# A 27,000-instruction block kernel: modulation vector built in column halves, later modulation tiles in six places, second attention in single visits

## What is computed

```python
cond = jax.nn.silu(c)
for i in range(2):
    mod = (cond @ ada_w[i] + ada_b[i])                  # ada_w[i]: 1024 x 6144
    sh1, sc1, g1, sh2, sc2, g2 = jnp.split(mod, 6)      # twelve vectors of 1024 in all
    h = rmsnorm(x, norm1_g[i]) * (1 + sc1) + sh1
    y = sliding_window_sink_attention(...) if i == 0 else stick_breaking_attention(...)
    x = x + g1 * y
    h = rmsnorm(x, norm2_g[i]) * (1 + sc2) + sh2
    x = x + g2 * swiglu(h, ...)
# first attention: window 128, softmax with one sink logit per head, 16 query heads, 2 key heads
# second: s = q k / 8, a = sigmoid(s) * prod over later keys of sigmoid(-s); o = a v
```

## Time and profile before

| | us |
|---|---|
| median of three runs | 2427.55 |
| lowest, highest | 2424.36, 2430.35 |
| the profiled execution, whole | 2431.22 |
| its span, first to last instruction | 2429.4 |
| PE busy in it | 2314.1 (95%) |
| DVE busy | 1227.2 (51%) |
| ACT busy | 874.0 (36%) |
| POOL busy | 201.6 (8%) |

### The profile page before, as it was taken

The page is one execution under the profiler, slowest core; times in us unless marked ns, Lnnn a source line. Parts: engine busy times, 40 slices in busy tenths (PEclk is TensorE's granted clock), DMA queues, the critical chain, the costliest instruction groups (busy, mean ns, idle before and its releaser), DMA issues.

```text
span 2429.4 us, 27096 instructions
## 1 busy us (share of the span) xinstructions
PE 2314.1 (95%) x10968; PEld 1830.4 (75%) x10968; DVE 1227.2 (51%) x1761; ACT 874.0 (36%) x1452; POOL 201.6 (8%) x146
## 2 busy tenths in 40 slices
PE   3888999999999999999999999999999999999998
PEld 2555778888876767888887887767768887888887
DVE  6787556453346564433334546456654335553453
ACT  1554322222244443331232224553653323332332
POOL 6200100000100001000001000121120001000001
PEclk9998899999999999999999999999999999999999
DMA  6333255552221211323222322212123222232222
GB/s 250 117 116 128 68 182 203 178 214 91 99 73 53 70 53 52 105 96 102 98 96 78 98 101 88 104 62 70 61 87 108 96 100 79 96 104 96 87 95 78
DMA packets 70973, 250.91 MB, mean 103 GB/s; under 512 B 7872, under 2 KB 8000, under 8 KB 70848
## 3 DMA queue, kind: packets, MB, share of 16 engines
q1 hardware_dynamic: 70848, 249.17, 30.0%
HBM read 244.95 MB, written 4.19 MB: 103 GB/s over the span
## 4 chain that ended last, share of the span: by engine, by line
PE 82%; DVE 8%; ACT 6%; issue 2%; POOL 1%; DMA 0%; SPq 0%; DVEq 0%; POOLq 0%; ACTq 0%
PE pb L717 24%; PE pb L721 24%; PE pb L719 24%; DVE slab L1317 2%; ACT whi L1026 1%; PE pb L762 1%; DVE wlo L1294 1%; PE pb L912 1%; PE pb L887 1%; DVE slab L1345 1%; ACT hhi L1054 1%; PE pb L739 1%; DVE hlo L1351 1%; PE pb L740 1%; PE pb L741 1%
## 5 line engine op out<-in xcount | busy, mean ns | idle before, releaser
L717 PE MATMUL pb<-hhi,whi 128*128 128x512 f32 x1976 | 799.8, 405 | 4.9 <-ACT hhi L1054 3.0
L1294 DVE TENSOR_TENSOR wlo<-raw,whi 128x1024 fp32r<-128x1024 f32 x361 | 449.5, 1250 | 678.2 <-ACT whi L1026 678.0
L719 PE MATMUL pb<-hhi,wlo 128*128 128x512 f32 x1976 | 774.7, 392 | 2.1 <-DVE wlo L1294 2.1
L721 PE MATMUL pb<-hlo,whi 128*128 128x512 f32 x1976 | 774.8, 392 | 0.7 <-DVE hlo L1351 0.7
L1026 ACT ACTIVATE whi<-raw 128x1024 fp32r<-128x1024 f32 x361 | 378.7, 1055 | 710.1 <-PE pb L721 674.8
L717 PEld LDWEIGHTS pb<-hhi,whi 128*128 128x128 f32 x1976 | 372.9, 189 | 114.8 <-issue 41.2
L721 PEld LDWEIGHTS pb<-hlo,whi 128*128 128x128 f32 x1976 | 372.7, 189 | 84.4 <-DVE hlo L1351 3.5
L719 PEld LDWEIGHTS pb<-hhi,wlo 128*128 128x128 f32 x1976 | 373.7, 189 | 78.8 <-issue 3.8
L717 PE MATMUL pb<-ahi,whi 128*128 128x512 f32 x848 | 336.8, 397 | 3.6 <-ACT ahi L1186 2.2
L721 PE MATMUL pb<-alo,whi 128*128 128x512 f32 x848 | 331.6, 391 | 0.0
L719 PE MATMUL pb<-ahi,wlo 128*128 128x512 f32 x848 | 331.3, 391 | 0.0
(11 more groups left out here) (198 smaller groups left out, 1809.1 us busy)
## 6 DMA issues: line engine op xcount, KB each, us to landing
raw<-stream SPq DMA_DIRECT2D x361, 512.0 KB, 3.2
slab<-ada_w SPq DMA_DIRECT2D x80, 512.0 KB, 4.5
early<-ada_w SPq DMA_DIRECT2D x16, 512.0 KB, 13.4
X<-xT SPq DMA_DIRECT2D x8, 256.0 KB, 6.8
ya<-slab SPq DMA_DIRECT2D x8, 256.0 KB, 2.5
slab<-ya SPq DMA_DIRECT2D x8, 256.0 KB, 4.8
outT<-X SPq DMA_DIRECT2D x8, 256.0 KB, 2.1
cst<-consts SPq DMA_DIRECT2D x1, 646.5 KB, 3.8
```

The costliest lines, as they stand in the source:

```text
L717: e.matmul(out, wh, hi, start=s.k == 0, stop=False)
L719: e.matmul(out, wl, hi, start=False, stop=False)
L721: i = e.matmul(out, wh, lo, start=False, stop=s.last)
L1294: e.tensor_tensor(wlo[:, u % NW, :], raw[:, u % NRAW, :], whi[:, u % NW, :].bitcast(F), ALU.subtract).then_inc(*v_cut.up(u))
```

## The change

- Start. The 16 tiles of j = 0, 1 are loaded as 32 half tiles (columns 0 to 511 of both, then columns 512 to 1023), each half with a sum and a `premod` of its own; the scale's products are all on DVE, of the shift's those with k = 0, 1, 2 are done by PE directly (`PRE_PE = 3`). The norm makes h 0 to 3 after the first half and h 4 to 7 after the second. The `late` constants are loaded apart, later. POOL does `pow` ahead of `first`.
- The first qkv group has six tiles (8, 9, 0, 1, 2, 3) where it had three; then 4, 5 and then 6, 7, and only the last pair has attention woven in. QSQ and QG have five places.
- Later modulation tiles have six places, two accumulators, and are taken elsewhere: eight in the first group's second half, one in every second round of the first attention (it was one place in the list in each round), 20 in the second half of the wo_a product, the others in the feed-forward part as before. `modsum(j - 1)` now stands behind the third tile of j.
- First attention: the negated maximum is made for both heads at once by two dependent operations, the sink's term by a third, and ACT needs one small exp where it had two; values alternates the two heads.
- Second attention: start, gather and turn stand together, then four steps.
- The cut kept back at the end of a product now stands behind `norm(n, 2)`; it stood ahead of the spread.

```diff
     def mods():
-        for j in range(12):
+        for j in range(2, 12):
             for k in range(KD):
+                if k == 3 and j > 2:
+                    tick("modsum", j - 1)
                 tick("fma", 8 * j + k)
                 yield 1
-            tick("modsum", j)
-            yield 1
+        tick("modsum", 11)
...
         for k in range(KD):
             tick("norm", n, k)
+            if k == 2 and s.kept:
+                s.cut(s.kept.pop())
...
-    run(some(mod, 9))
+    for k in range(4):
+        tick("pre", 0, k)
     tick("total", 0)
     tick("scaled", 0)
-    run(some(mod, 8))
+    tick("pow", 0)
     tick("first")
-    tick("pow", 0)
+    for k in range(4, KD):
+        tick("pre", 0, k)
     tick("spread", 0)
+    tick("premod", 0)
     s.cut(0)
-    run(some(mod, 1))
-    tick("angles")
-    for k in range(KD):
+    for k in range(4):
         tick("norm", 0, k)
         if k in (1, 3):
             s.cut((k + 1) // 2)
+    tick("angles")
...
-                next(mod, None)
+                if i % 2:
+                    next(mod, None)
...
-    run(group(8, 9, 0))
+    first = group(8, 9, 0, 1, 2, 3)
+    for k in range(4):
+        tick("pre", 1, 2 * k)
+        tick("pre", 1, 2 * k + 1)
+        run(some(first, 6))
+    tick("premod", 1)
+    for k in range(4, KD):
+        tick("norm", 0, k)
+    run(woven(first, some_mods(8), 3))
     tick("tables")
-    run(woven(group(1, 2), keys(), 2))
+    run(woven(group(4, 5), keys(), 2))
     side = queries()
-    for ts in ((3, 4), (5, 6), (7,)):
+    for ts in ((6, 7),):
...
-        run(gemm(src, K, outs(4), "m", evac=evac, hold=True))
+        last = gemm(src, K, outs(4), "m", evac=evac, hold=True)
+        run(last if ahead is None else woven(last, some_mods(20), 1.5))
...
         for i in range(4):
             tick("start", t, i)
-            yield 1
-            yield from advance()
+            advance()
             fly.append([(t, i), 0])
+            yield 3
...
+        def pre(half, k):
+            w.wait_ge(a_att, "cond")
+            w.wait_ge(d_early[half, k], "in")
+            for j in (1, 0) if k >= PRE_PE else (1,):
+                a, o = early_part(half, k, j), modacc[j][:, S * half:S * half + S]
...
-            for h in range(2):
-                m = e.tensor_scalar(nm[:, h:h + 1], mx[:, h:h + 1], nr[:, 2 * i + h:2 * i + h + 1], nsinks[:, 2 * t + h:2 * t + h + 1],
-                                    ALU.mult, ALU.min)
-            m.then_inc(*v_att.up(("nm", t, i)))
+            e.tensor_tensor(nm, mx, nr[:, 2 * i:2 * i + 2], ALU.mult).then_inc(*v_att.up(("top", t, i)))
+            w.wait_ge(v_att, ("top", t, i))
+            e.tensor_tensor(nm, nm, nsinks[:, 2 * t:2 * t + 2], ALU.min).then_inc(*v_att.up(("nm", t, i)))
+            w.wait_ge(v_att, ("nm", t, i))
+            e.tensor_tensor(es, nm, W("sinks", 2 * t, 2), ALU.add).then_inc(*v_att.up(("es", t, i)))
```

More of the change, by code:

```diff
@@ L45 @@
 CONST, NCONST = spans([
-    ("ident", 128), ("maskA", 256), ("late", 512), ("maskB", 128),
-    ("maskS", 128), ("perm", 128), ("heads", 2), ("one", 1), ("invf", 1), ("sgn", 1), ("half", 8),
+    ("ident", 128), ("maskA", 256), ("maskB", 128),
+    ("maskS", 128), ("perm", 128), ("heads", 2), ("one", 1), ("invf", 1), ("sgn", 1), ("half", 8), ("late", 512),
 ])
@@ L192, in rstd @@
         tick("scaled", sid)
-        while s.kept:
-            s.cut(s.kept.pop())
         tick("pow", sid)
@@ L237, in keys @@
             yield 1
+        tick("query", 0)
+        yield 1
     done = set()
@@ L1339, in norm @@
             w.wait_ge(t_norm, ("spread", n))
[L1340 removed]
+            if n == 0:
+                w.wait_ge(v_mod, ("half", k // 4))
+            elif k == 0 and shift is not None:
                 w.wait_ge(v_mod, mg)
```

160 lines of the change are left out of this document (102 added, 58 removed).

## The result

| | before | after |
|---|---|---|
| median, beside each other on one chip, five runs each | 2427.86 | 2437.53 |
| lowest, highest | 2424.36, 2431.88 | 2436.14, 2440.98 |
| ratio to before, 95% interval | | 1.0042 (1.0029 to 1.0054) |
| span of the profiled execution | 2429.4 | 2437.2 |
| mean granted clock in it | 0.983 | 0.978 |

The account below looks back on a forecast made before the run. PE and DVE bound the first attention by turns, PE nearly all the rest after it. Terms 2.4 - 15.5 + 7.5 - 7.1 - 3.5 - 12 + 1.9 = -26.3 gave a 2401 us median, range 2383 to 2424.

Parts of the forecast that it names:

- 1. The start: Up to the first scores: +2.4 us, scores at 100.1 us, with 24 steps more done by then.
- third rival: No change, 2426 us, chance 0.10: attention gives nothing and the start is 10 us late through late raw units or angles.
- 2. The first attention: First scores to last values: -15.5 us, near DVE's bound, from fewer modulation operations and cuts.
- second rival: The attention gives nothing, 2416 us, chance 0.17: every burst of four steps stops DVE at a cut.
- fourth rival: Slower, 2437 us, chance 0.08: with less filler PE idles between items and the first attention's granted clock falls.
- my bound for PE: First attention: PE's savings in steps, visits and a modulation sum would give -23 us.
- 3. The second half of wo_a: Last values to norm 1: +7.5 us, 33.5 us in all, as DVE becomes the bound.
- My upper bound of +14: Second half of wo_a: at most +14 us, if all DVE operations are slowed like cuts beside POOL's sums.
- 4 and 5: Behind the second norm, -7.1 us from stall, slow sum and slow steps; then -3.5 us from five sums instead of seven.
- 6. The second attention: Second attention, 28 rounds: -12 us, of it -5.6 from single visits and -6 from waits; range -4 to -15.
- 7. The kept cut: Cut moved inside the norm, between h 2 and h 3: +1.9 us, range 0 to 6.
- The alternate heads: Values of the first attention with alternating heads: worth nothing, eight records staying at 0.66 us.

Follow-up runs that it names:

- e4: Kernel after without the range reduction of the rotary angles on POOL: 2427.93 us, ratio 1.0007 to before.
- e9: Kernel after with the first qkv group cut back from six tiles to three: 2430.46 us, ratio 1.0014 to before.
- e12: Kernel of e1 with 32 modulation products in the first attention where it has 16: 2423.94 us, ratio 0.9990 to before.
- e15: Kernel after with the first attention's cuts made due by wo_a bursts placed behind the next round of items: 2438.26 us, ratio 1.0047 to before.
- e16: Kernel of e14 with the first attention's cuts a round later, as in e15: 2411.61 us, ratio 0.9940 to before.
- e14: Kernel of e13 with POOL's angles begun ahead of the variance's power and the first modulation sum ahead of the spread: 2408.05 us, ratio 0.9925 to before.
- e1: Kernel after with 4 modulation products in wo_a's second half instead of 20, the others in the feed-forward part: 2417.12 us, ratio 0.9961 to before.
- e3: Kernel after with the statistics of tiles 4 to 6 in wo_a's second half one step later, behind the cut: 2431.71 us, ratio 1.0014 to before.
- e2: Kernel before with only the single visits of the second attention taken over: 2420.24 us, ratio 0.9976 to before.
- e7: Kernel after with the kept cut put back ahead of the spread, as before: 2436.83 us, ratio 1.0032 to before.
- e11: Kernel after with three tiles first, statistics behind the cut, and 10, 8, 10 products in start, attention, wo_a: 2411.40 us, ratio 0.9926 to before.
- e13: Kernel of e11 with 4, 16 and 8 products in start, first attention and wo_a's second half: 2411.55 us, ratio 0.9934 to before.

## Why the prediction was wrong, by its own steps

**1. The start (+2.4 forecast, +13.9 found): the term was mis-sized, by some 7 us in the price of DVE's operations beside POOL and by 4 in the path behind h 4.** The times up to 47 us are close: DVE's eight products end at 27.9 (27), PE's first product starts at 35.5 (34), DVE is at 47.9 (45). The step that failed is "eight products at 0.87 us (L1303, the same width, beside a busy POOL)" carried to the 13 products and three cuts of half 1, to end at 60, and the 1.6 us for product and rounding of an h. The 13 products took 13.8 us where the sum had 11.3, two low halves before them 1.8 each where an undisturbed one takes 0.75, and the cut among them 1.62 (the one of 2.28 ran behind the last product, beside PE's sum, and delayed nothing). So the last product ended at 64.2 (58.6 forecast), and with the slow small operation and low half behind it PE began h 4 at 70.9 where the sum had 63.5: 7.4 of the 11.5 us, 0.7 of it a slower sum of PE. The other 4.0 lie between there and the first scores (24 steps +1.2, evacuation and sine +0.6, keys' spread +0.8, from there to the scores +1.4), they are the same in e4, and no run takes them apart. e4 takes POOL's work away and brings 10.0 us back, more than the 7.4, since its products at 0.68 are below the price of the sum as well.
The row that should have told me was the earlier trace rows: cut 0 took 2.30 us there, against 1.22 in the earlier trace rows. I had seen it and took 1.5 as a value between. And the six operations from which I took 0.87 ran beside operations of POOL with one input alone (10.57 to 15.13 us, before); the two-input ones, which cost DVE three times as much (last section), began at 17.08. My third rival had a start ten us late as well, but for raw units that come late, and for these PE never waited here.

**2. The first attention (-15.5 forecast, -9.3 found): mis-sized, and the shared bound misread.** Its parts, as the runs price them: 13 products fewer at 0.79 to 0.87 us, -11 (I had -15.5 for them); the dependent small operations +1.9 (I had +6); the 24 steps and the fewer cuts 0 to +0.5 (I had -3.1 for cuts on DVE's side and -16.4 on PE's). I took a value near DVE's bound because DVE is the fuller engine. But neither is the bound for long: 24 steps more for PE in the same stretch (e9) cost nothing, and a product more for DVE costs two thirds of itself (e12). My second rival, "the attention gives nothing", named a reason, a burst of four steps that stops DVE at a cut: the waits at cuts did rise, from 15.7 to 22.3 us. e15 and e16 don't show that these waits carry a price of their own, so what holds the stretch stays open between them and the chain from stage to stage. The clock, my fourth rival, took a part too: 42 of 129 block matmuls of the attention run slow after, against 37 of 201 before (durations of 0.55 us and more in the timelines), so the share that PE does slowly rose; in e14 it is 21 of 201. PE's busy time fell by 15.7 us where my bound for PE had -23. Filler in this stretch is paid back in part by a higher clock (0.91 in e9 against 0.85), and no run separates that from the waits it fills.

**3. The second half of wo_a (+7.5 forecast, +22.4 found): mis-sized, in the waits between DVE's operations.** That DVE becomes the bound was right, as e1 shows with 1.29 us for each product. The step that failed is "35.4, less 2.4 since starts lie closer", which with 33.5 in all leaves DVE 0.5 us of waits. Measured in the stage of 50.3 us: DVE busy 37.3 (cuts at 1.53 and one product of 1.75 beside POOL's sums), 6.8 of ladder behind ACT, 2.1 ahead of its first operation, 2.0 for the last products of PE, and 2.1 in small gaps and behind the last residual. The ladder's 6.8 us stood in the earlier trace rows, at the same four cuts; what I missed is that a wait that costs nothing beside a full PE is added in full once DVE is the bound. e3 removes most of the ladder and gives 5.2. My upper bound of +14 was for slowed operations alone; it had no term for the order of ACT's queue, where the next cut stands behind a square that needs the residual, which DVE does after five products.

**4 and 5** (-10.6 forecast together, -9.6 found) were right: no wait for a sum behind norm 1 is left, and e12, which moves 16 products ahead of the norm, gets 5.1 us more there.

**6. The second attention (-12 forecast, -10.6 found; -9.8 in e2) came out near by luck.** I had 5.6 for the visits and 6 for the waits. From the first start to the last gather the kernel after takes 194.7 us where before takes 203.1, as e2 does: the visits gave 8.3, and the waits nothing, since they moved from the gather to the start. The other 2.2 us are a slow stretch behind norm 2 that the profiled execution of the kernel before has and that of the kernel after doesn't. For the visits I had two values, up to 0.3 us a round by the delayed matmuls of the earlier trace rows, and 0.1 by the rule of the Trainium skill, TensorEngine Tiling (Array Packing), Key Properties, that a change of tiling mode drains the engine, since one change of four goes; I took 0.2. The runs show 0.30, with three of the four changes left: the delayed matmuls give the size, and the count of changes doesn't.

**7. The kept cut** (+1.9 forecast): 0.9 over the whole hybrid part, 0.7 in e7.

**The alternate heads** (0 forecast): 0 found.

The first and the third term together were 26.4 us off, the second 6.2. The side that I named as slower, a falling clock at 0.08, isn't what turned the sign.

## What to carry to other kernels

Filler work that an engine has room for by its busy share is not free where that engine's queue holds operations that others wait for: here a product of 1.28 us cost 1.3 to 1.65 in the start and 0.8 to 0.9 in the attention, while in the last stage the first ten cost 4.4 us together (27.9 before, 32.3 in e11) and the next ten 1.28 each (45.1 in e3). The small prices don't follow the count alone: eight cost 5.9 in e13 and 7.6 in e14, where the clock of the stage is 0.95 and 0.86. So price filler place by place, and share it out by the free time of each: with 4, 16 and 8 products instead of 8, 16 and 20, three tiles first and the statistics behind the cut, the changed kernel went from 0.4% slower to 0.7% faster than before.
Before work goes ahead of a residual, look at what the other engines have queued behind it; a short operation in ACT's order made DVE wait 1.7 us in each unit.

## What the runs showed of the hardware that I had not expected

Work of POOL slows DVE's operations on SBUF data by far more than I had assumed: four half-width products 2.73 us without it and 4.47 beside it (1.64 times), a cut up to 2.28 against 1.22, a 128 x 4 operation 1.05 against 0.16. What decides is which operation POOL does. These are operations of DVE and what POOL did then, the first four in the kernel after, the last from the kernel before (L1729 and L1660 add two tensors, L1725 has one input):

```profile
35.39 1.27 POOL L1729 TENSOR_TENSOR slab<-slab 128x512 f32<-128x512 f32 x1
35.41 1.80 DVE L1418 SCALAR_TENSOR_TENSOR hlo<-slab,small,hhi 128x512 fp32r<-128x512 f32 x1 [0.79 <-ACT hhi L1102]
42.60 1.50 POOL L1725 TENSOR_SCALAR slab<-slab 128x512 f32<-128x512 f32 x1
43.48 0.75 DVE L1418 SCALAR_TENSOR_TENSOR hlo<-slab,small,hhi 128x512 fp32r<-128x512 f32 x1 [0.79 <-ACT hhi L1102]
...
48.51 1.26 POOL L1660 TENSOR_TENSOR slab<-slab 128x512 f32<-128x512 f32 x1
```

In the start of the kernel after, nine operations of DVE on SBUF data begin during an L1729, the 128 x 4 one, the cut of 2.28 and the L1370 of 1.54 among them, and each takes 0.8 to 1.1 us longer than without POOL. Of the 22 that begin during an operation of POOL with one input none loses more than 0.45, and many nothing. Operations that read PSUM lose nothing beside either.
The Trainium skill, SBUF — State Buffer (SBUF: two separate sides), says that the two engines share a pair of ports as an exclusive lock for a whole instruction, taken by a DVE operation with two SBUF inputs or in a two-port mode, and that the other engine waits meanwhile. That fits the rows beside POOL's two-input operations, where the loss is about what is left of an operation of 1.3 us. It doesn't fit those beside one-input operations: the low half at 43.48 begins with 0.6 us of L1725 left and loses nothing, and the largest loss of the 22 (0.44, a product begun at 24.0) came with 1.5 us of POOL's operation left. For a sum, then, the price is what is left of a two-input operation of POOL, up to 1.1 us for each operation of DVE that meets one, and not a factor on its own time; my sum used a factor.

A visit to tiles of another shape between PE's steps costs about 0.15 us: taking two of three visits away saved 0.30 us a round, over 28 rounds, with all of these rounds at a granted clock of 1.00.
